# Five moves in the order of work of a two-layer transformer block with a mixture of experts

## What is computed

```python
def moe_ffn(h, w_router, router_bias, w_eg, w_eu, w_ed, w_sg, w_su, w_sd):
    scores = jax.nn.sigmoid((h @ w_router).astype(jnp.float32))
    ...                                        # group-limited top 8, weights wts
    # tokens are listed by expert, in blocks of 128 rows; row_tok, row_w, block_e
    def expert_block(args):
        tok, e = args
        xb = h_pad[tok]
        return (jax.nn.silu(xb @ w_eg[e]) * (xb @ w_eu[e])) @ w_ed[e]
    ...
    shared = (jax.nn.silu(h @ w_sg) * (h @ w_su)) @ w_sd
    return routed + shared

for i in range(DEPTH):
    mod_lat = (jax.nn.silu(c) @ w_mod[i] + b_mod[i])[:, None, :]
    ...
    x = x + gt1 * y_lat
    f_lat = (rmsnorm(x, g_ffn[i]) * (1 + sc2) + sh2).reshape(B * S, D)
    x = x + gt2 * moe_ffn(f_lat, *moe_args).reshape(B, S, D)
return rmsnorm(x, g_final)
```

## Time and profile before

| | us |
|---|---|
| median of 3 runs | 3411.73 (3403.13 to 3413.61) |
| the profiled execution | 3439.47 |
| its span, first to last instruction | 3437.7 |
| TensorE busy (matmul) | 3139.2, 91% |
| DVE, ScalarE, GpSimd busy | 1734.8, 1369.1, 676.9 |
| mean granted TensorE clock | 0.971 of full |
| DMA moved | 703.54 MB |

### The profile page before, as it was taken

The page is one execution under the profiler, slowest core; times in us unless marked ns, Lnnn a source line. Parts: engine busy times, 40 slices in busy tenths (PEclk is TensorE's granted clock), DMA queues, the critical chain, the costliest instruction groups (busy, mean ns, idle before and its releaser), DMA issues.

```text
span 3437.7 us, 49036 instructions
## 1 busy us (share of the span) xinstructions
PE 3139.2 (91%) x14864; PEld 2222.2 (65%) x14864; DVE 1734.8 (50%) x2570; ACT 1369.1 (40%) x1977; POOL 676.9 (20%) x757
## 2 busy tenths in 40 slices
PE   6999999999997999999999599999997899999995
PEld 3457877899545666666666346876863666666663
DVE  1354471222354666666666426462334566666665
ACT  2253351221224555555555325352212555555553
POOL 0000300000061323333332000020004332333331
PEclk9999999999998999999999799999998899999997
DMA  6420113333318999999999510112233999999994
GB/s 223 124 86 7 53 49 100 129 129 135 138 59 300 345 350 345 343 351 354 349 346 324 172 51 1 34 56 87 82 123 110 334 346 335 339 341 335 328 328 145
DMA packets 223715, 703.54 MB, mean 205 GB/s; under 512 B 55651, under 2 KB 104197, under 8 KB 169429
## 3 DMA queue, kind: packets, MB, share of 16 engines
q1 hardware_dynamic: 176356, 601.80, 47.2%
q0 software_dynamic: 47248, 100.21, 10.9%
HBM read 669.89 MB, written 98.31 MB: 223 GB/s over the span
## 4 chain that ended last, share of the span: by engine, by line
PE 61%; DMA 20%; issue 8%; DVE 6%; ACT 2%; SPq 2%; DVEq 1%; POOLq 0%; ACTq 0%; POOL 0%
DMA ring<-in_w_exp_up 8%; PE ps L826 7%; DMA region_v<-in_w_exp_up 6%; PE ps L907 6%; PE ps L833 6%; PE ps L834 6%; PE ps L835 6%; PE ps L855 5%; DMA region_k<-in_w_exp_up 4%; PE ps L1105 4%; PE ps L878 4%; PE ps L880 3%; PE ps L879 3%; PE ps L1010 3%; PE ps L1031 3%
## 5 line engine op out<-in xcount | busy, mean ns | idle before, releaser
L878 PE MATMUL ps<-region_h_split,region_q_split 128*128 128x512 f32 x846 | 350.1, 414 | 71.6 <-DVE region_q_split L1530 36.2
L1958 POOL DMA_INDIRECT acc<-region_q,idx_out x141 | 226.3, 1605 | 925.0 <-DVE region_q L1570 816.7
L1536 DVE TENSOR_TENSOR ring_split<-ring,region_h_split 128x1024 fp32r<-128x1024 f32 x210 | 246.8, 1222 | 251.5 <-ACT region_h_split L1172 241.0
L855 PEld LDWEIGHTS ps<-con,region_c 128*128 128x128 f32 x1686 | 221.2, 167 | 145.9 <-DVE region_c L1543 74.3
L1172 ACT ACTIVATE region_h_split<-ring 128x1024 fp32r<-128x1024 f32 x210 | 210.1, 1052 | 240.5 <-DMA ring<-in_w_exp_up 197.6
L835 PE MATMUL ps<-region_x_split,ring_split 128*128 128x384 f32 (+2 forms) x800 | 282.9, 354 | 0.0
L855 PE MATMUL ps<-con,region_c 128*128 128x128 f32 x1686 | 258.9, 282 | 25.9 <-DVE region_c L1543 17.5
L907 PE MATMUL ps<-ring,region_c 128*128 128x512 f32 x560 | 252.0, 593 | 1.0 <-DVE region_c L1548 1.0
L1172 ACT ACTIVATE region_q<-ps 128x512 f32<-128x512 f32 (+1 forms) x163 | 106.8, 655 | 347.7 <-PE ps L907 232.3
L878 PEld LDWEIGHTS ps<-region_h_split,region_q_split 128*128 128x128 f32 x846 | 162.5, 192 | 120.5 <-issue 90.5
L879 PE MATMUL ps<-ring_split,region_q_split 128*128 128x512 f32 x560 | 220.2, 393 | 0.0
(11 more groups left out here) (315 smaller groups left out, 6870.4 us busy)
## 6 DMA issues: line engine op xcount, KB each, us to landing
ring<-in_w_exp_gate SPq DMA_DIRECT2D x70, 1024.0 KB
ring<-in_w_exp_up SPq DMA_DIRECT2D x70, 1024.0 KB
ring<-in_w_exp_down SPq DMA_DIRECT2D x70, 1024.0 KB
ring<-in_w_mod SPq DMA_DIRECT2D x24, 2048.0 KB, 8.0
region_k<-in_w_exp_gate SPq DMA_DIRECT2D x36, 1024.0 KB
region_k<-in_w_exp_up SPq DMA_DIRECT2D x36, 1024.0 KB
region_k<-in_w_exp_down SPq DMA_DIRECT2D x36, 1024.0 KB
region_v<-in_w_exp_gate SPq DMA_DIRECT2D x35, 1024.0 KB
```

What stands on the lines that cost most here:

```text
L855: last = nc.tensor.transpose(ps[0:t.shape[1], at:at + t.shape[0]], t, ident[0:t.shape[0], 0:t.shape[0]])
L878: mm(m_gu[s], xT_hi[s][:, k, :], high, start=k == 0, stop=False)
L1536: tt(wgu_lo[w][:, :, 2 * c:2 * c + 2, :], wgu[w][:, :, 2 * c:2 * c + 2, :], wgu_hi[c], ALU.subtract).then_inc(sl["w_lo"], 1)
L1958: pool.indirect_dma_start(ACC[s], bass.IndirectOffsetOnAxis(ap=idx_out[:, s:s + 1], axis=0), yb[:, s, :], None, bounds_check=TOK - 1, oob_ ...
```

## The change

Five moves. (1) SyncE loads the small vectors of both layers and then the tokens ahead of the first modulation panel. (2) Each shared row tile is stored by ScalarE: it waits for its own copy and issues the DMA on its queue; `store_shared` goes. (3) The lists are loaded by GpSimd, once `listed` is complete, ahead of its waits for the stored token rows. (4) TensorE does not wait for all five engines before the gate broadcast, but for the last output copies of ScalarE (`y_a`) and DVE (`y_b`). (5) In a turn ScalarE and DVE do `tokens` of the next block ahead of `weights_of` of the next block, and SiLU and `hidden` ahead of both; the same holds ahead of the loop.

```diff
--- before.py
+++ after.py
@@ -651,7 +651,10 @@
                     at += rows
                 assert at == NVEC
 
-            load_vectors(0)
+            for l in range(DEPTH):
+                load_vectors(l)
+            sp.dma_start(XT[:, 0:CT, :], ctx[0].rearrange("(t p) d -> p t d", p=P)).then_inc(s_x, 16)
+            sp.dma_start(XT[:, CT:NT, :], x[0].rearrange("(t p) d -> p t d", p=P)).then_inc(s_x, 16)
             def kpn(w, a, b):
                 return w[:, a:b].rearrange("(k p) n -> p k n", p=P)
 
@@ -710,12 +713,6 @@
                     load_panel(done[0])
                     done[0] += 1
 
-            load_until(("mod", 0, 0))
-            sp.dma_start(XT[:, 0:CT, :], ctx[0].rearrange("(t p) d -> p t d", p=P)).then_inc(s_x, 16)
-            sp.dma_start(XT[:, CT:NT, :], x[0].rearrange("(t p) d -> p t d", p=P)).then_inc(s_x, 16)
-            load_until(("mod", 0, 1))
-            for l in range(1, DEPTH):
-                load_vectors(l)
             load_until(("mod", 0, 3))
             sp.dma_start(mask_in, mask).then_inc(s_mask, 16)
             for l in range(DEPTH):
@@ -741,11 +738,6 @@
 
                 sl = L[l]
 
-                def store_shared(n):
-
-                    after(sp, "sd", l, A[n])
-                    sp.dma_start(ACC[0][A[n] * P:A[n] * P + P, :], yb[:, n % 2, :]).then_inc(s_sh[n % 2], 16)
-
                 sp.wait_ge(filled, names["o", l, A[-1]].fill)
                 sp.wait_ge(tab_ready, l + 1)
                 n_blocks = sp.value_load(tab[0:1, 2 * TABN:2 * TABN + 1], min_val=1, max_val=max_blocks(l))
@@ -767,12 +759,6 @@
                 for n in range(2):
                     load_gate_up(expert(n), n)
                     load_down(expert(n), n)
-                for n in range(2):
-                    store_shared(n)
-                sp.wait_ge(sl["listed"], 16 * TOPK * len(A))
-                sp.dma_start(slots, LISTS[l].rearrange("(p n) a -> p (n a)", p=P)).then_inc(sl["list_in"], 16)
-                for n in range(2, len(A)):
-                    store_shared(n)
                 sp.wait_ge(filled, names["sd", l, A[-1]].fill)
                 for n in range(2, DEPTH_W):
                     load_gate_up(expert(n), n)
@@ -909,6 +895,7 @@
                                 last.then_inc(sl["dn_done"], 1)
                             with pe.If(n < n_blocks):
                                 turn_hidden(s, n)
+                return n_blocks
 
             pe.wait_ge(s_con, 16)
             fills = []
@@ -1157,9 +1144,10 @@
                     for before in fills[-3:]:
 
                         pe.wait_ge(drained[before.drain], before.count)
-                    moe(a[0])
+                    n_blocks = moe(a[0])
                     loop_end(pe)
-                    pe.wait_ge(loops_done, 5 * (a[0] + 1))
+                    for emptied in ("y_a", "y_b"):
+                        pe.wait_ge(L[a[0]][emptied], n_blocks + 1)
                 if job.drain:
                     last.then_inc(filled, 1)
 
@@ -1196,19 +1184,18 @@
 
                 act.sem_inc(sl["y_a"], 1)
                 tokens(0, 1)
-                weights_of(1, 1, 0)
                 silu(0, 1)
                 tokens(1, 2)
+                weights_of(1, 1, 0)
                 with act.Fori(0, max_turns(l) // UNROLL) as m:
                     with act.If(UNROLL * m < n_blocks):
                         for r in range(UNROLL):
                             n, s = UNROLL * m + r + 1, (r + 1) % 2
-                            with act.If(n + 1 < n_blocks):
-                                weights_of((r + 2) % UNROLL, m + (r + 2) // UNROLL + 1, n)
                             with act.If(n < n_blocks):
                                 silu(s, n + 1)
                             with act.If(n + 1 < n_blocks):
                                 tokens(1 - s, n + 2)
+                                weights_of((r + 2) % UNROLL, m + (r + 2) // UNROLL + 1, n)
                             with act.If(n <= n_blocks):
                                 act.wait_ge(sl["dn_done"], n)
                                 act.wait_ge(sl[f"scat{1 - s}"], 16 * (UNROLL // 2 * m + r // 2 + 1))
@@ -1387,7 +1374,9 @@
                     n = active(l).index(a[1])
                     if n >= 2:
                         act.wait_ge(s_sh[n % 2], store_no(l, n) - 16)
-                    last = copy(yb[:, n % 2, :], ps)
+                    copy(yb[:, n % 2, :], ps).then_inc(drained["act"], 1)
+                    act.wait_ge(drained["act"], job.count)
+                    act.dma_start(ACC[0][a[1] * P:a[1] * P + P, :], yb[:, n % 2, :]).then_inc(s_sh[n % 2], 16)
                 elif kind == "moe":
                     moe(l)
                     loop_end(act)
@@ -1550,20 +1539,19 @@
                 dve.sem_inc(sl["y_b"], 1)
                 weights_of(0, 0)
                 tokens(0, 1)
-                weights_of(1, 1)
                 hidden(0, 0, 0)
                 tokens(1, 2)
+                weights_of(1, 1)
                 turned_hidden(0, 0)
                 with dve.Fori(0, max_turns(l) // UNROLL) as m:
                     with dve.If(UNROLL * m < n_blocks):
                         for r in range(UNROLL):
                             n, s = UNROLL * m + r + 1, (r + 1) % 2
-                            with dve.If(n + 1 < n_blocks):
-                                weights_of((r + 2) % UNROLL, n + 1)
                             with dve.If(n < n_blocks):
                                 hidden(s, (r + 1) % UNROLL, n)
                             with dve.If(n + 1 < n_blocks):
                                 tokens(1 - s, n + 2)
+                                weights_of((r + 2) % UNROLL, n + 1)
                             with dve.If(n <= n_blocks):
                                 dve.wait_ge(sl["dn_done"], n)
                                 dve.wait_ge(sl[f"scat{1 - s}"], 16 * (UNROLL // 2 * m + r // 2 + 1))
@@ -1927,6 +1915,8 @@
                         store_gates(n - 2, A[n - 2])
                     if n >= 3:
                         store_lists(n - 3, A[n - 3])
+                pool.wait_ge(sl["listed"], 16 * TOPK * len(A))
+                pool.dma_start(slots, LISTS[l].rearrange("(p n) a -> p (n a)", p=P)).then_inc(sl["list_in"], 16)
                 for s in range(2):
                     for q in (s_h, s_w):
                         pool.wait_ge(q[s], store_no(l, len(A) - 2 + s))
```

## The result

The changed kernel took 3386.9 us (median of 6 runs, 3382.7 to 3390.9), against 3411.3 for the kernel before on the same chip: ratio 0.9929, 95% interval 0.9914 to 0.9943. That is 24 us faster, inside the range on record, and less than half of the 51 us that I forecast.

The account below looks back on a forecast made before the run. The prediction took TensorE as the bound in the mixers and part of the expert loop, with late weight loads over DMA in other turns. Gains of 5 + 20.5 + 0.5 + 25 = 51 us took 3411.7 to 3361, range 3333 to 3391.

Parts of the forecast that it names:

- A: Start: small vectors and tokens loaded ahead of the first modulation panel; 5 us faster, bounds 2 and 6.
- B: Expert loop entries: ScalarE stores shared rows, GpSimd loads lists; 20.5 us faster, 8.5 in layer 0, 12 in layer 1.
- C: Gate broadcast, started without the barrier of all engines: 0 to 1 us in layer 0, 0 in layer 1; 0.5 taken.
- D: Expert loop turns: next tokens ahead of next weights on ScalarE and DVE; 25 us faster, bounds 5 and 55.
- shifts along: Start: everything behind the first modulation row, panel reloads included, moves earlier with it; 4.6 to 6 us, 5 taken.
- GpSimd issues them when the list stores have landed, by about 2647.5, even with the first expert loads: Layer 1 entry: the list loads go out level with the first expert loads; a step towards 12 us gained.
- rival 3: Loop entries: lists and stores land behind expert loads, B falls to 10 with D at 20: 3376; chance 0.07.
- land hardly earlier than the copy did: Combining after the loops: loads of the sums still wait for the barrier, so 0 to 1 us gained in layer 0.
- on-time turn: Expert loop turn in which TensorE is back to back: forecast to grow from 10.04 by about 0.2, to 10.25 us.
- the lead: Late expert loop turn, from weights landing to first gate/up product: forecast to fall from 7.49 to 2.4 us.
- my floors: Expert loop turns: shortest by full DMA share, 10.78 us in layer 0, 10.36 in layer 1; TensorE's is 10.25.
- rival 1: Expert loops: idle DMA is uneven engine load that earlier requests cannot fill; D is 6, sum 32, 3380; chance 0.22.

Follow-up runs that it names:

- entry_only: Kernel before with only the entry moves (shared rows stored on ScalarE's queue, lists loaded by GpSimd): 3407.7 us, ratio interval 0.9988 to 1.0005.
- no_turn_order: Changed kernel with weights taken ahead of tokens again in each turn, as in the kernel before: 3403.8 us, ratio 0.9975.
- one_piece_first: Changed kernel with the first of four weight pieces rounded ahead of SiLU and tokens, three behind: 3389.1 us, ratio 0.9932.
- again: The kernel before, unchanged, run and profiled a second time: 3411.6 us, ratio 0.9998.
- start_only: Kernel before with only vectors and tokens loaded ahead of the first modulation panel: 3407.7 us, ratio 0.9992.
- turn_order_only: Kernel before with only the turn order changed, next tokens ahead of next weights on ScalarE and DVE: 3392.3 us, ratio 0.9940.
- held: Changed kernel, with SyncE waiting for the first gathered rows before loading experts 2 and 3: 3381.3 us, ratio 0.9908.
- early_loads: Changed kernel, with the next buffer's gate/up weights requested ahead of the wait for the down product: 3377.0 us, ratio 0.9898.

## Why the prediction was right or wrong

The parts by the table (without the first trace), each as the mean of kernels without it less that of kernels with it. A, by the first mixer product: 2.7. B, by the entries (entry_only, no_turn_order, changed and one_piece_first against again, start_only and turn_order_only): 4.8 in layer 0, -4.3 in layer 1. C, by the stretch between the loops: 677.3 less 675.4, 1.9. D, by the loops (turn_order_only, changed and held against the five in the old order): 8.4 in layer 0, 10.6 in layer 1. The sum is 24.1; the measured gain is 24.3. That they agree so well is luck: the stretch from the first mixer product to layer 0's first shared product, which no part's edit touches, differs between these traces by 5 us (910.3 to 915.5).

**The frame, half wrong.** I took the gain off profile and median alike, for want of a row that says where the profile is long. The trace had them: idle times put down to "issue" and "remote" at both entries (10.24 in the earlier trace rows, and the four lines under **again**), the very places from which part B was read. I left the 10.24 in and took its neighbours for typical. They were not.

**A, 5 forecast, 2.7 found.** The first row came 4.65 earlier, as worked out. The step that failed is "shifts along": three more panels at 5.4 us and the clock come behind it. I had 2 as the lower bound for that reason.

**B, 20.5 forecast, 0.5 found.** This is the error. Layer 0: 8.5 forecast, 4.8 found; the idle term was 7.33 in the first trace and 3.74 in the second, and with the second trace's rows the same sum is 3.74 + 3.05 (6.72 - 3.67, clock) - 1.5 = 5.3. Layer 1: 12 forecast, -4.3 found. The first step that failed is "GpSimd issues them when the list stores have landed, by about 2647.5, even with the first expert loads". It issued the list load 14.4 us behind the first expert load (2617.18 against 2602.74). The cause stands in GpSimd's last list store of layer 1. In the first trace of before, where the first expert load is at 2647.94:

```profile
2644.21 0.96 POOL L1918 DMA_INDIRECT slot_list<-choices,place  x1 [0.30 <-issue]
```

In the second, where that load is at 2616.79:

```profile
2625.02 0.95 POOL L1918 DMA_INDIRECT slot_list<-choices,place  x1 [0.30 <-issue]
```

ScalarE's stalls had given GpSimd time to finish 3.7 ahead of the loads; otherwise it finishes 8.2 behind them. Counted from layer 1's first shared product, that store is at 55.4 in the first trace and at 53.9 in the second, the first expert load at 59.1 and 45.6: the loads came late, not the stores early. So against the second trace DVE has the list only 1.2 us earlier, counted from layer 1's first shared product (66.8 instead of 68.0): hardly a gain, but no loss. The second step that failed makes the loss: I priced the list load but gave the gathers behind it no cost. Experts 2 and 3, now 12 us behind the first loads instead of 30, put another 6 MB in front of them; the first gather landed 8.4 behind its issue, and 4.0 in held, where these loads wait for it and entry 1 is 3.7 shorter. This is my rival 3 (7%), in layer 1 alone and larger than I had it: B was to fall to 10, and fell to 0.5.

The Trainium skill's rule that I had set against the move, DMA: Bandwidth & Descriptors, "Issuing engines are not separate DMA queues", is that a DMA started from another engine saves only time to issue. The traces agree: on GpSimd's queue the list took 6.7 us from issue to DVE, on SyncE's 8.8 (2630.36 to 2639.15), beside expert loads either way. What I said there of the trace was misread: in the kernel before, layer 1's first shared row is issued behind the loads of experts 0 and 1 (2652.26 against 2647.94), not before them.

**C, 0.5 forecast, 1.9 found.** DVE starts combining 15.1 us behind layer 0's last output copy instead of 16.8 to 17.4, now released by the loads of the sums: the step "land hardly earlier than the copy did" was too low by some 1.5. Layer 1's end has not moved (43.5 to 43.9 in all).

**D, 25 forecast, 19.0 found**, and the on-time turn (10.17 found, 10.25 forecast) and the lead (2.37 against 2.4) as worked out; the DMA share rose as forecast, by 0.01 to 0.02. One term was misread: the reload is issued 1.46 us into the turn (1116.04 - 1114.58), not 1.9, and three turns come to 32.5. The mechanism that I had priced, fuller DMA engines in every turn, is the smaller part. From turn 15 to turn 60 it is 2.3 us in layer 0 and 5.5 in layer 1, by the means over the same kernels, where half way to my floors would have been some 7 and 15; the transfers have grown by nearly as much as the lead has shrunk. The rest is had once a loop: 3.8 and 4.3 in the first 15 turns, where lateness now sets in at the 12th turn instead of the 9th, and 4.4 and 1.5 behind turn 60 (in layer 0 3.6 of it in the last five turns); the first turn itself is 2.0 and 0.7 longer. So my rival 1 (22%) was nearer to the mechanism, "the DMA rate as it is": from turn 15 to 60 the rate went from 348 to 350 GB/s in layer 0, but from 336 to 341 in layer 1, where half of that layer's gain comes from. It sized D at 6, since it counted the end of a loop and not its beginning. That my 25 came near was luck.

## What to carry to other kernels

When the one profiled execution is longer than the timed ones, find its idle times without a releaser first, and read no term from beside them: they do not only add time, they change which of two chains is late. Before a wait in front of large loads is removed, follow the small transfers (lists, then gathers) that go behind those loads. In a loop bound by bytes, an earlier request or a shorter lead is won at the start and once at the end; in each turn it wins only what the DMA rate can still rise (here 0.05 us a turn in layer 0, 0.12 in layer 1). And before two single traces are compared stage by stage, look at the granted clock of each stage: here it was worth up to 3 us in a loop's first turn.

## What was unexpected of the hardware

- One execution was 27 us longer than a second one of the same kernel at two places (101.9 and 92.8 against 88.8 and 78.7), with idle times of ScalarE there that have no releaser and that the second lacks. What caused them stays open.
- The DMA share is no measure of what is left: window 1150 to 1850 moved 350 GB/s at share 0.97 in early_loads and 351 at 0.99 in the changed kernel, with the same steady turn.
- The 16 small matmuls of a modulation row took 3.64, 3.64, 3.64 and 3.49 us in the changed kernel and 1.92 in the second row of start_only, in the same order of work, with the clock column at 1.00 in both. In the changed kernel that 1.00 says nothing: its trace has no record of the clock ahead of 44 us (start_only's begin at 26), and without a record the column stands at 1.00. Where there is one, column and duration agree (0.66 beside 3.48).
